# Norm, projection and recurrence in two groups of tiles: the first before the tokens, the second between them

## What is computed

```python
xn = rmsnorm(x, g_mix)
xr, gate, q, k, v = split(xn @ w_in)           # w_in is 1024 x 2560
xc = causal_conv(xr, width 4)                  # needs the 3 tokens before
h_t = a_t * h_(t-1) + u_t                      # RG-LRU; a and u from two block-diagonal gates of xc
y_rnn = h * gelu(gate)
y_attn = three dilated windows of q, k, v      # the sample group attends to a cache of 2048 rows
x = x + [rmsnorm(y_rnn); rmsnorm(y_attn)] @ w_out
x = x + peer(rmsnorm(x))                       # per token: 128 of 16384 experts, a row of expert_u
                                               # and a row of expert_v each, 1024 wide
y = rmsnorm(x)
```

## Time and profile before

| | |
|---|---|
| median of 3 runs | 3788.25 us (3784.18 to 3790.95) |
| the profiled execution's own time | 3790.84 us |
| its span in the profile | 3789.1 us |
| busy over the span: PE, DVE, ACT, POOL | 62%, 55%, 12%, 54% |
| mean granted clock of PE, as a share of 2.4 GHz | 0.743 |
| moved by all transfers | 1250.65 MB, of it 1107.43 MB by POOL's gathers |

### The profile page before, as it was taken

How to read it: one execution, slowest core, us unless ns; L and a number is a source line. 1 busy time by engine, 2 the same in 40 slices (tenths; PEclk the granted TensorE clock), 3 DMA queues, 4 the chain that set the end, 5 groups by cost and what they waited for, 6 DMA issues and landing times. The chain is left out here.

```text
span 3789.1 us, 32751 instructions
## 1 busy us (share of the span) xinstructions
PE 2343.8 (62%) x10360; PEld 807.8 (21%) x10360; DVE 2084.0 (55%) x5182; ACT 465.5 (12%) x729; POOL 2039.5 (54%) x2135
## 2 busy tenths in 40 slices
PE   6999576676656666455494656645665575466554
PEld 4664332121112222111231101200110121012000
DVE  2251337987955556233264844764575467447641
ACT  2330521000022222000120000000000000000000
POOL 0000012576766667444364766776677667767773
PEclk8999787797777777666697856856875686668555
DMA  2114333899999999999799999999999999999996
GB/s 76 30 56 146 110 132 150 310 403 390 391 379 400 393 391 394 365 373 363 261 378 359 400 391 399 393 389 396 393 393 396 390 395 394 395 399 390 389 409 244
DMA packets 379204, 1250.65 MB, mean 330 GB/s; under 512 B 44586, under 2 KB 77546, under 8 KB 376732
## 3 DMA queue, kind: packets, MB, share of 16 engines
q0 software_dynamic: 304128, 1107.43, 75.7%
q1 hardware_dynamic: 74908, 141.16, 10.4%
HBM read 1214.74 MB, written 33.69 MB: 329 GB/s over the span
## 5 line engine op out<-in xcount | busy, mean ns | idle before, releaser
L1671 DVE CUSTOM_DVE_ANT_0 u_rows<-u_rows,xb 128x1024 f32<-128x1024 f32 x1056 | 1269.5, 1215 | 1145.3 <-PE xb L1603 856.4
L1534 POOL DMA_INDIRECT v_rows<-expert_v,idx_v x1056 | 1008.4, 955 | 653.8 <-PE y_acc L1623 376.5
L1525 POOL DMA_INDIRECT u_rows<-expert_u,idx_u x1056 | 1011.0, 957 | 498.0 <-issue 265.0
L1623 PE MATMUL y_acc<-v_rows,w_row 128*32 128x512 f32 x4224 | 839.6, 936 | 695.8 <-DMA v_rows<-expert_v,idx_v 694.2
L1603 PE MATMUL xb<-parts,pick 48*128 48x512 bf16 x2112 | 474.1, 456 | 369.2 <-DVE dots L1671 362.9
L1623 PEld LDWEIGHTS y_acc<-v_rows,w_row 128*32 128x32 f32 x4224 | 166.7, 146 | 1088.6 <-issue 1088.6
L1809 PE MATMUL pair<-arena 128*128 128x512 f32 x576 | 328.9, 672 | 57.1 <-DMA arena<-w_query_by_group 57.1
L1603 PEld LDWEIGHTS xb<-parts,pick 48*128 48x128 bf16 x2112 | 98.8, 97 | 988.9 <-DVE dots L1671 586.3
L368 PE MATMUL zp<-xT,w 128*128 128x352 f32 x768 | 230.4, 463 | 6.2 <-DMA w<-w_in 6.2
L368 PEld LDWEIGHTS zp<-xT,w 128*128 128x128 f32 x768 | 147.3, 192 | 88.7 <-issue 8.6
L1638 ACT ACTIVATE acts<-dots 128x32 f32<-128x32 f32 x33 | 7.6, 229 | 1220.3 <-DVE dots L1671 1220.3
(11 more groups left out here) (277 smaller groups left out, 2035.1 us busy)
## 6 DMA issues: line engine op xcount, KB each, us to landing
u_rows<-expert_u,idx_u POOLq DMA_INDIRECT x1056, 9.9
v_rows<-expert_v,idx_v POOLq DMA_INDIRECT x1056, 9.8
arena<-w_query_by_group SPq DMA_DIRECT2D x8, 2048.0 KB, 18.4
arena<-cache_kT SPq DMA_DIRECT2D x8, 1792.0 KB, 14.5
w<-w_in SPq DMA_DIRECT2D x16, 512.0 KB, 3.8
arena<-cache_v SPq DMA_DIRECT2D x8, 1024.0 KB, 21.6
z_far<-zT SPq DMA_DIRECT2D x3, 2112.0 KB, 11.7
parts<-x_parts SPq DMA_DIRECT2D x396, 16.0 KB
```

The source lines that it names most:

```text
L1525: nc.gpsimd.indirect_dma_start(self.u_rows[:, n % U_SLOTS, :], None, a["expert_u"][0], bass.IndirectOffsetOnAxis(ap=self.idx_u[(b + 1) % 2 ...
L1534: nc.gpsimd.indirect_dma_start(self.v_rows[:, n % V_SLOTS, :], None, a["expert_v"][0], bass.IndirectOffsetOnAxis(ap=self.idx_v[b % 2][:, t ...
L1623: last = nc.tensor.matmul(self.acc[g * TB:(g + 1) * TB, half:half + HALF], self.w_row[:, b % 2, lo:lo + TB], self.v_rows[:, (TB * b + n) % ...
L1671: nc.vector.tensor_tensor_reduce(out=self.u_rows[:, n % U_SLOTS, :], in0=self.u_rows[:, n % U_SLOTS, :], in1=self.xb[:, n % XB_SLOTS, :], ...
```

## The change

`normed_T` and the old `project` go. A new `project` does norm, products, convolution, gates and recurrence for a list of tiles: called for tiles 0 to 3 ahead of the tokens (with the masks, now in class `Masks`), and again for tiles 4 to 7 and the sample between the tokens, after the routing of tile 3. Between the calls the convolution's last three inputs and the last state are kept in `c.tail` and `c.last`. `w_in` is therefore read twice; the host lays it out by blocks, so that a partition's 4 KB are one run, and lays the cache of values out so that a partition's four groups are one run. The gate weights go to DRAM once and are loaded in each call. The parts of a stage get weights (`cost`), the steps of the stages are shared out anew, and each stage between the tokens first does `LEAD` = 12 steps after issuing its loads, before its first part. Cut to its core:

```diff
-def constants(nc, a, c):
+def constants(nc, a, c, far):
...
+            sp.dma_start(far.wgate, c.wgate[:].rearrange("p g t i -> p (g t) i")).then_inc(gates_stored, 16)
+            sp.wait_ge(gates_stored, 16)
...
-def normed_T(nc, a, c, xnT):
...
-def project(nc, a, c, xnT, zT, v_tok, far):
...
-    def __init__(self, tok, first, last, parts):
-        self.tok, self.first, self.last, self.parts = tok, first, last, parts
+    def __init__(self, tok, first, last, cost, lead=0):
+        self.tok, self.first, self.last = tok, first + lead, last
+        self.reached = list(accumulate(cost))
 
     def upto(self, m):
-        return self.first + (self.last - self.first) * (m + 1) // self.parts
+        if m < 0:
+            return self.first
+        return self.first + (self.last - self.first) * self.reached[m] // self.reached[-1]
...
+    def sp(self, sp):
+        sp.wait_ge(self.mask_done, 1)
+        for x, whole in enumerate((self.mult, self.bias)):
+            sp.dma_start(self.far.mask[x], whole).then_inc(self.stored, 16)
+        sp.wait_ge(self.kept, 1)
+        for x, (some, new) in enumerate(((self.s_mult, self.n_mult), (self.s_bias, self.n_bias))):
+            for b in range(DB):
+                rows = slice(NS * (b % 4), NS * (b % 4) + NS)
+                sp.dma_start(self.far.s_mask[x, b // 4, rows, 0:self.c.SK], some).then_inc(self.stored, 16)
+                sp.dma_start(self.far.s_mask[x, b // 4, rows, self.c.SK:], new[:, b, :]).then_inc(self.stored, 16)
...
+def project(nc, a, c, far, stage, tiles, take, banks, pace_of, masks):
+    NT = len(tiles)
+    sample = tiles[-1] == PT
+    first = tiles[0] == 0
+    TP = (NT - 1) * P if sample else NT * P
...
+    KINDS = "xgqk"
...
+    for k in range(NT):
+        for x in range(2):
+            place(("N", k, x), 2)
+    for t in range(CC):
+        for kind in KINDS:
+            for ch in range(NCH):
+                place((kind, t, ch), 5)
+        for g in range(2):
+            for ch in range(NCH):
+                place(("G", t, g, ch), 2)
+    for k in range(NT):
+        place(("V", k), 6)
+        place(("K", k), 2)
+    if sample:
+        place("L", 2)
+    pace = pace_of(cost)
...
+        x_in, xn, stat = take("x_in", [P, 2, D]), take("xn", [P, D]), take("stat", [P, 2, 4])
+        xnT, w, wv = take("xnT", [P, KC, T]), take("w", [P, 3, KC * P]), take("wv", [P, KC, DR])
...
+            def load_w(o):
+                if o >= 3:
+                    kind, t = KINDS[(o - 3) % 4], (o - 3) // 4
+                    ring.filled(sp, at[kind, t, NCH - 1])
+                sp.dma_start(w[:, o % 3, :], a["w_in_tiles"][o]).then_inc(w_landed[o % 3], 16)
+
+            load_x(0)
+            load_x(1)
+            for o in range(3):
+                load_w(o)
+            sp.dma_start(wgate, far.wgate).then_inc(wgate_landed, 16)
+            pace.sp(sp, -1)
+            n = 0
+            for k in range(NT):
+                for x in range(2):
...
+                    if kind == "k" and t:
+                        sp.wait_ge(c_done, t)
+                        sp.dma_start(far.z[0, t - 1, :, over], xr[:, (t - 1) % 2, :]).then_inc(y_stored, 16)
...
+                sp.wait_ge(q_ready, t + 1)
+                sp.dma_start(far.z[1, t, :, over], qz[:, t % 2, :]).then_inc(q_stored, 16)
+                sp.wait_ge(k_ready, t + 1)
+                sp.dma_start(far.z[2, t, :, over], kT[:, t, :]).then_inc(k_stored, 16)
+            if masks:
+                masks.sp(sp)
+            sp.wait_ge(c_done, CC)
+            sp.dma_start(far.z[0, CC - 1, :, over], xr[:, (CC - 1) % 2, :]).then_inc(y_stored, 16)
...
+            for t in range(CC):
+                for o, kind in enumerate(KINDS):
+                    use = 4 * t + o
+                    pe.wait_ge(w_landed[use % 3], 16 * (use // 3 + 1))
+                    for ch, (lo, hi) in enumerate(CHUNKS):
+                        n = at[kind, t, ch]
+                        ring.room(pe, n)
+                        for k in range(KC):
+                            last = nc.tensor.matmul(ring.bank(n)[:, 0:hi - lo], w[:, use % 3, k * P:(k + 1) * P], xnT[:, k, lo:hi],
+                                                    start=(k == 0), stop=(k == KC - 1))
+                        last.then_inc(ring.made, 1)
+                        pace.pe(pe, n)
+                if t == 0:
+                    pe.wait_ge(wgate_landed, 16)
+                pe.wait_ge(xc_ready, t + 1)
+                for g in range(2):
+                    for ch, (lo, hi) in enumerate(CHUNKS):
+                        n = at["G", t, g, ch]
+                        ring.room(pe, n)
+                        nc.tensor.matmul(ring.bank(n)[:, 0:hi - lo], wgate[:, CC * g + t, :], xc[:, lo:hi],
+                                         start=True, stop=True).then_inc(ring.made, 1)
+                        pace.pe(pe, n)
+            pe.wait_ge(wv_landed, 16)
+            pe.wait_ge(k_ready, CC)
...
+            pace.dve(dve, -1)
+            if first:
+                coefficients(nc, c, dve, then)
+            for k in range(NT):
+                root(k)
+                for x in range(2):
+                    pace.dve(dve, at["N", k, x])
+                    turned(k, x)
+            if masks:
+                masks.dve(dve)
+            for t in range(CC):
+                pass_over("x", t)
+                if t:
+                    gated(t - 1)
+                pass_over("g", t)
+                conv(t)
+                if t:
+                    spread(t - 1)
+                pass_over("q", t)
+                pass_over("k", t)
+                if t:
+                    scan(t - 1)
+                for x in range(2 * NCH):
+                    pace.dve(dve, at["G", t, x // NCH, x % NCH])
+            gated(CC - 1)
+            spread(CC - 1)
+            scan(CC - 1)
...
-                if t < 4:
-                    src = a["cache_v"][0, G * r:G * (r + 1), PAST - HALF:PAST].rearrange("g (p i) h e -> i p g (h e)", i=4)[t]
-                else:
-                    src = a["cache_v"][0, G * r:G * (r + 1), 0:PAST - HALF].rearrange("g (p i) h e -> i p g (h e)", i=16)[t - 4]
+                src = a["cache_v_near"][r, t] if t < 4 else a["cache_v_old"][r, t - 4]
...
+            pace.sp(sp, -1)
...
-ROUTE_STEPS = 52
+LEAD = 12
+ROUTE_STEPS = 44
+PROJECT_STEPS = 108
+ATTEND_STEPS = 120
+SAMPLE_STEPS = 32
+MERGE_STEPS = 48
...
+                project(nc, a, c, far, "project_early", early, Arena(arena).take, banks, still, masks)
...
+        begins = ROUTE_STEPS * (WAVE - 1)
+
+        def paced(steps):
+            return lambda cost: Pace(tok, begins, begins + steps, cost, LEAD)
...
+            if r == WAVE:
+                return Pace(tok, begins, begins + LEAD + ROUTE_STEPS, [1] * RSTEPS, LEAD)
+            return Pace(tok, P * (r - 1) + TB, P * (r - 1) + TB + RSTEPS, [1] * RSTEPS)
...
+        project(nc, a, c, far, "project_late", late + [PT], Arena(arena).take, banks, paced(PROJECT_STEPS), None)
+        begins += PROJECT_STEPS
...
+        attend(nc, a, c, far, "attend_late", late, yaT, taken.take, banks, paced(ATTEND_STEPS))
+        begins += ATTEND_STEPS
...
+    laid["cache_v_near"] = near["cache_v"].reshape(DB // 4, 4, 4, P, DR).transpose(0, 2, 3, 1, 4)
+    laid["cache_v_old"] = old["cache_v"].reshape(DB // 4, 4, DT, Consts.OLD, DR).transpose(0, 2, 3, 1, 4)
+    w_in = _np.asarray(laid.pop("w_in"))[0]
+    by_tile = w_in[:, :4 * DR].reshape(KC, P, 4, CC, P).transpose(3, 2, 1, 0, 4)
+    laid["w_in_tiles"] = by_tile.reshape(4 * CC, P, KC * P)
+    laid["w_v"] = w_in[:, 4 * DR:].reshape(KC, P, DR).transpose(1, 0, 2)
```

More of the change, by code:

```diff
@@ L20 @@
 from contextlib import ExitStack
+from itertools import accumulate
 import concourse.bass as bass
@@ L1788, in _ @@
                     tok.sp_begin(sp)
+                pace_of(tiles[0]).sp(sp, -1)
                 for r in tiles:
@@ L1836, in _ @@
                 c_ident = self.ident[:]
+                pace_of(tiles[0]).pe(pe, -1)
                 for r in tiles:
@@ L1983, in _ @@
                 nc.vector.tensor_copy(opt, self.opt_i)
+                pace_of(tiles[0]).dve(dve, -1)
                 for r in tiles:
@@ L2021, in program @@
     far = Far(nc, c)
-    still = lambda parts: Still()
+    still = lambda cost: Still()
     early, late = list(range(WAVE)), list(range(WAVE, PT))
@@ L2045, in program @@
             banks = [s2.ps(f"bank{i}", [P, HALF])[:] for i in range(8)]
+            with ExitStack() as ctx3:
+                take = lambda name, shape, dt=F32: ctx3.enter_context(nc.sbuf_tensor(name, shape, dt))[:]
+                masks = Masks(nc, c, far, s2, take)
+                project(nc, a, c, far, "project_early", early, Arena(arena).take, banks, still, masks)
             with ExitStack() as ctx3:
@@ L2056, in program @@
         router.ident = c.ident
-        def paced(first, last):
-            return lambda parts: Pace(tok, first, last, parts)
+        begins = ROUTE_STEPS * (WAVE - 1)
```

(15 more changed lines are left out.)

833 lines of the change are left out of this document (433 added, 400 removed).

## The result

The changed kernel takes 3664.35 us (median; 3655.49 to 3673.15), the kernel before 3787.98 in the same comparison: a ratio of 0.967 [0.966, 0.968], 124 us less. The span is 3660.6 us, 128.5 shorter than before.

A forecast was written before the change was run, and what follows sets the result against it. Products bound the front to 649 us, DMA the rest to 3710. Front -180 and between the tokens +80 (48 + 10 + 11 - 16 - 14 + 11 + 30) give -100: median 3688 us, range 3645 to 3738.

The forecast's parts named there:

- The front: Stretch before early attention: forecast shorter by 180 us (165 to 190), early attention starting at 203 us instead of 382.69.
- the front gains less: Rival: mask stores on SP delay v and k, and the one-slot norm costs more: 25 us, so 3713; chance 0.10.
- The end of one more stage and the late projection's stalls: Between the tokens: +11 us (8 to 12) for barrier and drain, +30 for stalls (bounds 2 to 53).
- the clock: Rival: late projection runs at PE clock 0.75, so PE bounds it; 34 us longer, 3722; chance 0.15.
- tokens stand still: Rival: part of the late projection holds every engine and no gather runs beside it; 3829 us; chance 0.03.
- no stalls: Rival: the late projection runs as attention did, 28 us less, 3660; chance 0.10.
- `LEAD`: -16: Opening of `merge`: twelve steps run under the loads DVE waited for, returning 16 us (-16 to 0).
- the sample and `merge` get fewer steps ... nothing, up to 6: Sample's stage and `merge`: same loads over fewer steps, PE staying at 86%; cost nothing, up to 6 us.
- it does not do what it says: Rival: twelve steps don't cover the opening's loads, 16 us not returned, 3704; chance 0.02.
- The cache of values: -14: Sample's cache reads: runs of 8 KB taken as quick as the gathers, saving 14 us (-14 to 0).
- no dip in the sample's reads: Sign expected in the profile after: the sample's reads of its cache show no dip in DMA rate.
- I am wrong if the tail's rate changes: Stated condition for failure: the long tail was to keep its rate, 2.69 us per token.

## Why the prediction was right, and where it was not

**The front** (-180, -176). The steps hold; the norm and the products with the wait for the masks took 6 us more, the close 2 less. The rival "the front gains less" falls.

**Bytes** (+48). 19 MB more between the tokens, as counted. Among the signs, "1269 MB moved in all" was a slip: x, z, k and v move from the front and are not new to the whole; the page has 1262.76, 12 more than before.

**Early routing** (+10): +10. **The end of one more stage and the late projection's stalls** (11 + 30): 34 in all; the stage took 374 us for the 365 foreseen, at clock 0.85 where 0.9 was expected and the clock rival had 0.75. PE busy 77% did not leave the tokens alone, but nothing stood still; the rivals "the clock", "tokens stand still" and "no stalls" fall. The 30 were put down for the norm and for four chains of convolution, gates and scan; three dips hold nearly all of the loss, at the first products behind the norm, at the last scan with v, and at the end.

**`LEAD`: -16, and "the sample and `merge` get fewer steps ... nothing, up to 6".** This is the step that failed. The opening is covered, as forecast, but each of its 12 steps is one that the parts lack: `merge`'s middle lost 30 us, and the stage as a whole came to +9 instead of -16 (+5 with the rings 64 off). The row 1900:2000 at 380 GB/s and PE 86% was read as slack for denser parts; with 60 steps instead of 48 `merge` regained 17 us, so its parts stood too close. The rival "it does not do what it says" falls, since the opening's loads are covered. Without the lead the time is the same: the term is worth 0.

**The cache of values: -14.** The layout is worth some 20 here, but attention and the sample together lost 7 more than before, not 3 less (1 more with the rings 64 off), and PE's wait for these loads rose from 3 to 16 us. The sign "no dip in the sample's reads" fails: slices of 4.6 us between 1624 and 1643 fall to 240 to 262 GB/s. The layout's sign was right; the term "nothing, up to 6" for fewer steps was too small, and why PE waits longer stays open.

**The tail's rate.** "I am wrong if the tail's rate changes": it did, and the sum held no step for where buffers lie. Without these 43 us the time is 3707 (the changed kernel with its rings 64 off), 19 above the forecast and still inside the range. By its terms these 19 are the front +5, `LEAD` and `merge` +21, attention and sample +4, the late projection -10 and early routing -1. So the mechanism of the front and of the bytes was right and the range holds without the alignment, but that the measured time came below the forecast and not above it was luck.

## What to carry to other kernels

When two kernels differ in allocations, compare a stretch whose code is the same in both before assigning the difference to the edit, and check where large gather buffers begin. When work is threaded between DMA-bound steps in a hand-written order, a busy share under 80% is not room: attention at 74% fell to 333 GB/s, the late projection at 77% to 366. Look for the longest run of one engine's work between two steps, as at v and at the first products of z; that shortening such runs pays is not shown, since doubling v's weight gained nothing. Steps given to one stage are taken from another: judge a lead or a share by the sum over the stages.

## What was not expected of the hardware

Gathers of 4 KB rows into a ring that begins 64 or 224 bytes past a multiple of 256 moved 392 to 394 GB/s in three kernels, into one on the multiple 401 to 402 in two: about 2% for either distance tried, and 41 to 43 us of a kernel of 3700.
